# Cross-attention in one block: the order in which x's norm, the keys, values and queries, the softmax and the output projection are issued

## The reference

```
h = h + memory_cross_attention(rmsnorm(h, xa_norm_w), rmsnorm(mem, mem_norm_w), wq, wk, wv, wo)

q, k, v = hn @ wq, mn @ wk, mn @ wv                    # 4 heads x 128
scores = einsum('bshd,bmhd->bhsm', q, k) * 128 ** -0.5
probs = softmax(scores, axis=-1)
o = einsum('bhsm,bmhd->bshd', probs, v)
return o @ wo
```

## Time and profile before

| what | us |
|---|---|
| median of three runs | 2760.13 (2759.71 to 2760.22) |
| the profiled execution | 2763.47 |
| its span | 2761.8 |
| PE busy | 2337.4 (85%) |
| DVE busy | 1330.7 (48%) |
| ACT busy | 807.1 (29%) |
| POOL busy | 21.5 (1%) |

### The profile page before, as it was taken

How to read it: one execution, slowest core, us unless ns; L and a number is a source line. 1 busy time by engine, 2 the same in 40 slices (tenths; PEclk the granted TensorE clock), 3 DMA queues, 4 the chain that set the end, 5 groups by cost and what they waited for, 6 DMA issues and landing times. The chain is left out here.

```text
span 2761.8 us, 40825 instructions
## 1 busy us (share of the span) xinstructions
PE 2337.4 (85%) x17264; PEld 1888.0 (68%) x17264; DVE 1330.7 (48%) x1528; ACT 807.1 (29%) x966; POOL 21.5 (1%) x62
## 2 busy tenths in 40 slices
PE   5996659978898798699999999996978577888885
PEld 5996559958776665699999999985854433443442
DVE  3763445565525301588888879784552211111112
ACT  4443223332113301443434334434441111111110
POOL 0000000000000000000000000000000000000000
PEclk9997879978758899899999999998999568999997
DMA  4442003410004430588888888863432399999998
GB/s 177 182 182 119 2 1 122 182 54 3 2 1 163 173 122 0 232 334 332 314 327 329 317 329 331 339 229 145 183 122 89 135 370 412 428 427 427 428 428 344
DMA packets 68156, 610.12 MB, mean 221 GB/s; under 512 B 9614, under 2 KB 9870, under 8 KB 16782
## 3 DMA queue, kind: packets, MB, share of 16 engines
q1 hardware_dynamic: 56906, 572.11, 51.8%
q0 software_dynamic: 1872, 23.07, 2.1%
q10 hardware_dynamic: 9216, 12.60, 1.3%
HBM read 674.85 MB, written 14.68 MB: 250 GB/s over the span
## 5 line engine op out<-in xcount | busy, mean ns | idle before, releaser
L1759 ACT ACTIVATE ffn_w_hi<-ffn_raw 128x2048 fp32r<-128x2048 f32 x128 | 245.0, 1916 | 371.2 <-PE psum L1804 367.9
L1766 DVE TENSOR_TENSOR ffn_w_lo<-ffn_raw,ffn_w_hi 128x2048 fp32r<-128x2048 f32 x128 | 292.3, 2287 | 88.9 <-ACT ffn_w_hi L1759 88.9
L1802 PE MATMUL psum<-u_hi,ffn_w_hi 128*128 128x256 f32 x1024 | 293.5, 287 | 15.1 <-DVE ffn_w_lo L1766 14.0
L2511 PE MATMUL psum<-moe_raw,moe_x_t 128*32 128x512 f32 x1536 | 219.3, 703 | 87.6 <-DMA moe_raw<-in_moe 80.0
L1804 PE MATMUL psum<-u_hi,ffn_w_lo 128*128 128x256 f32 x1024 | 293.0, 286 | 0.0
L1803 PE MATMUL psum<-u_lo,ffn_w_hi 128*128 128x256 f32 x1024 | 292.9, 286 | 0.0
L591 DVE SCALAR_TENSOR_TENSOR shared<-mod_raw,c_silu,shared 128x2048 f32<-128x2048 f32 x96 | 225.1, 2344 | 0.0
L1802 PEld LDWEIGHTS psum<-u_hi,ffn_w_hi 128*128 128x128 f32 x1024 | 199.8, 195 | 15.9 <-DVE ffn_w_lo L1766 14.2
L1803 PEld LDWEIGHTS psum<-u_lo,ffn_w_hi 128*128 128x128 f32 x1024 | 199.6, 195 | 0.4
L1804 PEld LDWEIGHTS psum<-u_hi,ffn_w_lo 128*128 128x128 f32 x1024 | 199.6, 195 | 0.0
L1802 PE MATMUL psum<-ffn_w_hi,ffn_hid_hi 128*128 128x512 f32 x512 | 199.5, 390 | 0.0
(11 more groups left out here) (537 smaller groups left out, 4491.2 us busy)
## 6 DMA issues: line engine op xcount, KB each, us to landing
moe_raw<-in_moe SPq DMA_DIRECT2D x96, 2048.0 KB, 17.4
ffn_raw<-in_ffn SPq DMA_DIRECT2D x128, 1024.0 KB, 5.0
ring<-in_stream SPq DMA_DIRECT2D x59, 2048.0 KB, 12.3
mod_raw<-in_mod SPq DMA_DIRECT2D x96, 1024.0 KB, 7.3
moe_raw<-in_moe POOLq DMA_DIRECT2D x48, 2048.0 KB
expert_rows<-moe_stage ACTq DMA_DIRECT2D x192, 64.0 KB, 8.4
x<-in_x SPq DMA_DIRECT2D x2, 1024.0 KB, 8.0
mem<-in_mem SPq DMA_DIRECT2D x2, 1024.0 KB, 15.0
```

The source lines that it names most:

```text
L1759: act.activation(self.w_hi[:, number % self.HIGHS], self.raw[:, number % self.RAWS], ACT.Copy)\
L1766: dve.tensor_tensor(self.w_lo[:, number % self.LOWS], self.raw[:, number % self.RAWS], self.w_hi[:, number % self.HIGHS].bitcast(F32), ALU ...
L1802: pe.matmul(out, lhs[0], rhs[0], start=start, stop=False)
L2511: mm = pe.matmul(summed(tile)[strip(q), :], e.x_t[:, tile // 4 % 2, UNIT_KC * u + c, strip(tile % 4)], w[:, c * COLS:(c + 1) * COLS], star ...
```

## The change

The block for the loads of `mem` goes: they are issued in the block after the RWKV rounds, into the buffer `u`, which the mixer no longer needs then and which now lives until cross-attention ends. The memory's norm stands alone and first. Everything else becomes one block.

In it, ACT squares x and takes the root ahead of its copies of the keys, and DVE makes the diagonals. After the keys PE multiplies a matrix of ones with the diagonals: the result (`factors`) holds each token's factor on every partition. In the loop over the values' 16 chunks PE also turns the two pieces of x of that chunk (plain transposes), into the banks 0 to 3, two chunks a bank; DVE multiplies each chunk from PSUM by the norm's weight and by `factors`. Before the queries PE waits until DVE has taken all of them. Then heads are staggered: a head's scores are issued after the next head's query, and so on, with ACT's and DVE's lists in the matching order. The output projection starts with the column groups 0 and 1, head by head, between the last turns and attends.

```diff
+def marks(first, *names):
+
+    return {name: first + n + 1 for n, name in enumerate(names)}
...
-    norm_turn(nc, k, x, h_t, lambda c: col(k, "xa_norm", c))
     norm_turn(nc, k, mem, mem_t, lambda c: col(k, "mem_norm", c), await_src=mem_in)
-    f0, t0 = k.ft, k.tt
+    f0, t0, o0, turns, HEADS = k.ft, k.tt, k.tt + 2, k.turns, range(XA_HEADS)
+    on_pe = marks(k.pe_n, "factors", "scores0", "scores1", "probs_t0", "scores2", "probs_t1", "o0", "scores3",
+                  "probs_t2", "o1", "probs_t3", "o2", "o3")
+    on_act = marks(k.act_n, "x0", "x1", "root", "exp0", "exp1", "probs_t0", "exp2", "probs_t1", "o0", "exp3", "probs_t2",
+                   "o1", "probs_t3", "o2", "o3")
+    on_dve = marks(s.n, "inv", "diag0", "diag1", "factors", "max0", "top0", "inv0", "probs0", "max1", "top1", "inv1",
+                   "probs1", "max2", "top2", "max3", "top3", "inv2", "probs2", "inv3", "probs3")
+    factors = h_t[:, KC - 1, :]
+    spare = bank(k, 4 + (t0 + 2) % 4)
...
+    def turned(c):
+        return bank(k, c // 2 % 4)[:, c % 2 * T:c % 2 * T + T]
     with nc.Block(no_gpsimd_drain=True) as block:
+            for j in range(2):
+                load_next(k, sp, STREAM["xo"][0] + j, k.tt_done, o0 + 8)
...
+            def query(h):
+                pe.wait_ge(k.ft_free, f0 + 4 + h + 1)
+                for c in range(KC):
+                    w = k.ring[:, (STREAM["xq"][0] + c // UNIT_KC) % SLOTS, c % UNIT_KC, h * P:(h + 1) * P]
+                    mm = pe.matmul(bank(k, h)[:, 0:T], w, h_t[:, c, :], start=c == 0, stop=c == KC - 1)
+                mm.then_inc(k.ft_done, 1)
+
+            def score(h):
+                pe.wait_ge(k.ft_free, f0 + 4 + 4 + h + 1)
+                for t in range(TT):
+                    mm = pe.matmul(scores(h)[:, t, :], q_t[:, h, t * P:(t + 1) * P], k_t[:, h, :], start=True, stop=True)
+                mm.then_inc(k.pe_sem, 1)
+
+            def turn(h):
+                pe.wait_ge(k.dve_sem, on_dve[f"probs{h}"])
+                for n in range(4):
+                    m, t = divmod(n, TT)
+                    mm = pe.transpose(bank(k, h)[:, n * P:(n + 1) * P], probs[:, h, t, m * P:(m + 1) * P], const(k, "ident"))
+                mm.then_inc(k.pe_sem, 1)
+
+            def attend(h):
+                pe.wait_ge(k.act_sem, on_act[f"probs_t{h}"])
+                for m in range(2):
+                    mm = pe.matmul(bank(k, h)[:, 0:T], v_m[:, m, h * P:(h + 1) * P], probs_t[:, h, m, :],
+                                   start=m == 0, stop=m == 1)
+                mm.then_inc(k.pe_sem, 1)
+
+            def out(n, h):
+                unit = STREAM["xo"][0] + h // 2
+                flat = k.ring[:, unit % SLOTS].rearrange("p k n -> p (k n)")
+                at = h % 2 * 4 * COLS + n * COLS
+                pe.wait_ge(k.act_sem, on_act[f"o{h}"])
+                for t in range(TT):
+                    if h == 0:
+                        pe.wait_ge(k.tt_free, o0 + 2 * n + t + 1)
+                    mm = pe.matmul(bank(k, 4 + (o0 + 2 * n + t) % 4), o_t[:, h, t * P:(t + 1) * P], flat[:, at:at + COLS],
+                                   start=h == 0, stop=h == XA_HEADS - 1)
+                    if h == XA_HEADS - 1:
+                        mm.then_inc(k.tt_done, 1)
             feature_group(k, pe, STREAM["xk"][0], mem_t, f0)
-            token_group(k, pe, unit_rows(STREAM["xv"][0], KC), mem_t, range(KC), t0)
-            feature_group(k, pe, STREAM["xq"][0], h_t, f0 + 4)
+            pe.wait_ge(k.dve_sem, on_dve["diag1"])
+            for t in range(TT):
+                mm = pe.matmul(spare[:, t * P:(t + 1) * P], const(k, "ones"), k.diag[:, t, :], start=True, stop=True)
+            mm.then_inc(k.pe_sem, 1)
+            for unit in range(2):
+                u = STREAM["xv"][0] + unit
+                pe.wait_ge(k.loaded[u % SLOTS], 16 * (u // SLOTS + 1))
+            for t in range(TT):
+                pe.wait_ge(k.tt_free, t0 + t + 1)
+            for c in range(KC):
+                w = k.ring[:, (STREAM["xv"][0] + c // UNIT_KC) % SLOTS, c % UNIT_KC, :]
+                for t in range(TT):
+                    mm = pe.matmul(bank(k, 4 + (t0 + t) % 4), mem_t[:, c, t * P:(t + 1) * P], w,
+                                   start=c == 0, stop=c == KC - 1)
+                    if c == KC - 1:
+                        mm.then_inc(k.tt_done, 1)
+                if c < 8:
+                    if c % 2 == 0:
+                        pe.wait_ge(k.ft_free, f0 + 4 + c // 2 + 1)
+                elif c % 2 == 0:
+                    pe.wait_ge(k.turn_taken, turns + c // 2 - 3)
+                for t in range(TT):
+                    mm = pe.transpose(turned(c)[:, t * P:(t + 1) * P], x[:, t, c * P:(c + 1) * P], const(k, "ident"))
+                if c % 2:
+                    mm.then_inc(k.turned, 1)
+            for unit in range(2):
+                u = STREAM["xq"][0] + unit
+                pe.wait_ge(k.loaded[u % SLOTS], 16 * (u // SLOTS + 1))
+            pe.wait_ge(k.turn_taken, turns + 8)
+            query(0)
+            query(1)
+            score(0)
+            query(2)
+            score(1)
+            turn(0)
+            query(3)
+            score(2)
+            turn(1)
+            attend(0)
+            score(3)
+            for unit in range(2):
+                u = STREAM["xo"][0] + unit
+                pe.wait_ge(k.loaded[u % SLOTS], 16 * (u // SLOTS + 1))
+            for h in range(3):
+                out(0, h)
+                out(1, h)
+                if h < 2:
+                    turn(h + 2)
+                attend(h + 1)
+            for n in range(2):
+                out(n, 3)
+            for n in range(2, 4):
+                for h in HEADS:
+                    out(n, h)
         @block.scalar
         def _(act):
-            for n in range(8):
+            def query(h):
+                act.wait_ge(k.ft_done, f0 + 4 + h + 1)
+                act.activation(q_t[:, h, :], bank(k, h)[:, 0:T], ACT.Copy).then_inc(k.ft_free, 1)
+
+            def exps(h):
+                act.wait_ge(k.dve_sem, on_dve[f"top{h}"])
+                for t in range(TT):
+                    exp = act.activation(probs[:, h, t, :], scores(h)[:, t, :], ACT.Exp, scale=P ** -0.5,
+                                         bias=top[:, h, t:t + 1], accum_out=total[:, h, t:t + 1])
+                exp.then_inc(k.act_sem, 1)
+
+            def turned_probs(h):
+                act.wait_ge(k.pe_sem, on_pe[f"probs_t{h}"])
+                act.activation(probs_t[:, h].rearrange("p m t -> p (m t)"), bank(k, h), ACT.Copy).then_inc(k.act_sem, 1)
+
+            def attended(h):
+                act.wait_ge(k.pe_sem, on_pe[f"o{h}"])
+                act.activation(o_t[:, h, :], bank(k, h)[:, 0:T], ACT.Copy).then_inc(k.act_sem, 1)
+            for t in range(TT):
+                act.activation(h_t[:, 8 * t:8 * t + 8, :].rearrange("p a b -> p (a b)"), x[:, t, :], ACT.Square,
+                               accum_out=k.ssq[:, t:t + 1]).then_inc(k.act_sem, 1)
+            act.wait_ge(k.act_sem, on_act["x1"])
+            act.activation(k.rms[:, 0:TT], k.ssq[:, 0:TT], ACT.Sqrt, bias=k.eps[:, 0:1], scale=1.0 / D).then_inc(k.act_sem, 1)
+            for n in range(4):
                 act.wait_ge(k.ft_done, f0 + n + 1)
-                act.activation((k_t, q_t)[n // 4][:, n % 4, :], bank(k, n % 4)[:, 0:T], ACT.Copy).then_inc(k.ft_free, 1)
+                act.activation(k_t[:, n, :], bank(k, n)[:, 0:T], ACT.Copy).then_inc(k.ft_free, 1)
+            query(0)
+            query(1)
+            exps(0)
+            query(2)
+            exps(1)
+            turned_probs(0)
+            query(3)
+            exps(2)
+            turned_probs(1)
+            attended(0)
+            exps(3)
+            turned_probs(2)
+            attended(1)
+            turned_probs(3)
+            attended(2)
+            attended(3)
+            s.eng = dve
+
+            def most(h):
+                dve.wait_ge(k.pe_sem, on_pe[f"scores{h}"])
+                s.step(dve.tensor_reduce(top[:, h], scores(h), AX.X, ALU.max))
+                s.settle()
+                s.step(dve.tensor_scalar(top[:, h], top[:, h], -P ** -0.5, None, ALU.mult))
+
+            def shares(h):
+                dve.wait_ge(k.act_sem, on_act[f"exp{h}"])
+                s.step(dve.reciprocal(total[:, h], total[:, h]))
+                s.settle()
+                s.step(dve.tensor_tensor(probs[:, h], probs[:, h], total[:, h].unsqueeze(2).broadcast_to([P, TT, T]),
+                                         ALU.mult))
+            dve.wait_ge(k.act_sem, on_act["root"])
+            s.step(dve.reciprocal(k.rstd[:, 0:TT], k.rms[:, 0:TT]))
+            s.settle()
+            for t in range(TT):
+                s.step(dve.tensor_scalar(k.diag[:, t, :], const(k, "ident"), k.rstd[:, t:t + 1], None, ALU.mult))
+            dve.wait_ge(k.pe_sem, on_pe["factors"])
+            s.step(dve.tensor_copy(factors, spare[:, 0:T]))
+            s.settle()
```

(99 more changed lines are left out.)

6 lines of the change are left out of this document (2 added, 4 removed).

## The result

| what | before | after |
|---|---|---|
| runs made together, median, us | 2760.18 (2759.71 to 2763.82) | 2731.68 (2730.85 to 2734.93) |
| ratio, 95% interval | | 0.9892 (0.9879 to 0.9905) |
| the profiled execution | 2763.47 | 2731.61 |
| its span | 2761.8 | 2729.9 |
| mixer's last add ends | 933.41 | 935.45 |

Faster by 28.5 us in the medians, by 26 to 33 in the ratio's interval; forecast was 25.0. The time, 2731.7 by the medians and 2730.4 by the ratio, lies at or under the range's lower end of 2731.0. Direction, mechanism and order of size were right; the size was too small.

The account below looks back on a forecast made before the run. PE was taken to bound the stage, with 33 us of bubbles from serial hand-overs. Terms 1.4 − 0.9 + 16.6 − 1.4 − 5.2 + 14.9 gave 25.4, taken as 25.0: 2738.5 us profiled, 2735.1 median; range 2731 to 2744.

Parts of the forecast that it names:

- Block gone, 1.4 us: Cross-attention's start: without the block for loading `mem`, ACT's first square starts where SP had started, saving 1.4 us.
- Two more issues upstream, −0.9: Block after the RWKV rounds: the two issues of `mem` there make every engine wait, costing 0.9 us.
- x's norm gone, 16.6: Front of cross-attention: one whole norm leaves the path ahead of the keys, saving 16.6 us.
- The remaining norm takes the slow place, −1.4: Memory's norm, now first: runs at the first place's lower clock (0.72 against 0.78), costing 1.4 us.
- Left on PE, −5.2: Keys to queries: factors product 0.4, 32 transposes 3.6 and the wait for DVE 1.2 add 5.2 us.
- rival C: Values' stretch: PE's clock falls to half, adding 31 us, 2766 us in all; chance 0.02.
- Queries with scores and a turn: Queries' stretch: 27.6 us of queries plus 2.2 us for two heads' scores and one turn; softmax keeps up.
- Tail, 14.9: Last query matmul's issue to the last add: 37.9 us instead of 55.0, less 2.2 moved into queries, gains 14.9.
- Rival B: Staggered heads: ACT's and DVE's in-order queues fail to overlap them, 9 to 10 us more, 2745 us; chance 0.07.
- Cold restarts, −0.4: Whole stage: 0.4 us taken off the gain for PE restarting cold behind five real waits.
- half-hidden transposes: Values' stretch, range's lower end: the transposes, charged 3.6 us, partly fit into gaps left by weight loads.
- a tail at its best: Softmax and output projection, range's lower end: gain up to its bound of 16 us instead of 14.9.

Follow-up runs that it names:

- change again: The changed kernel, unedited, timed again beside the kernel before: profiled at 2731.92 us, median 2732.71, ratio 0.9883.
- long series: The changed kernel, unedited, timed a third time beside two further edited versions on one chip: median 2733.24 us, ratio 0.9889.
- the late stage: The changed kernel plus 13 ACT copies in a block behind the stage, so the rest starts at its old time: median 2760.54 us, ratio 0.9992.

## Where the prediction was right, and which step failed

Each term, with the time of the profile after.

- *Block gone, 1.4 us.* ACT's first square came 936.29 − 935.45 = 0.84 us behind the last add; before, 935.62 − 933.41 = 2.21. That is 1.37.
- *Two more issues upstream, −0.9.* From DVE's last product of the RWKV rounds to ACT's first copy of the next block: 2.15 us before, 3.13 after. Measured −1.0. With the loads back in their block it is 2.14 again.
- *x's norm gone, 16.6.* One norm less, true in size. What I didn't name is that this term needs the early load. Before, x's norm covered the landing of `mem` (13.9 and 16.0 us after the issues, ahead of its first use at 952.23); without the edit priced at +1.4 − 0.9, 14.3 us would have stayed. The sum was right, the attribution was not: of two edits that only pay together I gave all to one.
- *The remaining norm takes the slow place, −1.4. This step failed.* From the first square to the keys took 951.78 − 936.29 = 15.49 us; I had 16.25 + 0.5 = 16.75. The norm itself took 14.97, 15.41 (change again) and 15.03 (long series): near the second norm of before (14.85), though it stands in the first one's place. The granted clock of the window is 0.79, where I expected 0.72 by the earlier trace rows. The sentence that failed is "The difference is the clock (...), which belongs to the place": one execution had two values of it, and I made the worse one a rule. By the norm alone that is −0.1 to −0.6 instead of −1.4. The second profile of the kernel before refutes the rule itself: there the first norm took 15.82 us and the second, in the good place, 16.25. Its row:

```profile
958.79 10.34 PE L208 MATMUL psum<-diag,mem 128*128 128x128 f32 x64 [6.26 <-DVE diag L191]
```

  The same 64 records took 8.95 us in that place in the first profile. Nor is it how long PE had rested: 9.01 us after 20.93 us of idle time in the kernel with the loads in their old block, 9.06 after 6.56 in the change, 10.34 here after 6.26. What sets the clock of one execution there stays open.
- *Left on PE, −5.2.* Keys with factors 951.78 to 979.92: 28.14 (forecast 28.1). Values with transposes to the first query 32.34 (32.3), in it the wait for DVE 1.17 (1.2). The transposes' price is shown by the doubled ones. I misread a chunk, though: "0.86 + 0.22 us of PE per chunk" should be 1.72 + 0.22, for 27.5 us by 16 chunks is 1.72, and the starts of two chunks lie 981.86 − 979.92 = 1.94 us apart. The slip only made DVE's margin look smaller than it is, and the transposes' share of the stretch is a ninth, not a fifth. The clock stood at 1.00 throughout, so rival C fell. By the rule of the Trainium skill, "TensorE: Matmul & The Clock Gate", Part 4, that transposes don't count as PE activity, a fall was possible; this trace, with a pair of transposes in every chunk for 31 us, shows none. At a ninth of the time this is a weak test of the rule; the stretch of transposes alone in the earlier trace rows speaks more directly against it.
- *Queries with scores and a turn*: 1012.26 to 1042.13 is 29.87 (29.8).
- *Tail, 14.9.* 1042.13 to the last add's end at 1080.28: 38.15 (37.9). Waits, with the drain, of 1.01 and three of about 0.65 (1.1 and three of 0.63). Rival B fell: no head waits for its probabilities.
- *Cold restarts, −0.4.* Not seen: the clock column is 1.00 in every window from 951.4, and queries and tail came within 0.3 us of the sum.

The stage gained 172.35 − 145.17 = 27.2 us; I had 26.3 in absolute times. Less 1.0 upstream, 26.2 against my 25.4, or 25.0 after the deduction. Of these 1.2, the failed step (16.75 − 15.49 = 1.3) and the deduction (0.4) make 1.7, and the tail (0.3) and the upstream part (0.1) take back 0.4. With the second profile of the kernel before (171.3) and the second of the change (145.6) the gain is 25.7, less 1.0 is 24.7: the sum itself was as good as two executions agree. That the next stage began at 1080.62, where I had 1080.4, was luck: the stage ran shorter than summed, and its start came 2.0 us later where I had 0.9.

The medians say more: 28.5, 31.4 and 29.1 us in the three series of the change beside the kernel before, each with an interval of 3.6 to 5.0 us to either side. What the traces place is 25 to 26 us. The 2 to 6 us above that were not found, and no step of the sum can be named for them: neither profiles compared like for like (26.9) nor the late stage settles them. The profiled "before" was 3.3 us over its median, and its experts 6 us slower than another profile of it, which shows how little one execution tells at this size.

And the range: its lower end of 2731.0 allowed 4 us under the forecast, filled by errors of terms alone: 1.4 us for the norm, which came, and some 3 us for half-hidden transposes and a tail at its best, which did not. Runs of one kernel spread over 8 us, and medians of a few runs over 3 (2731.68, 2732.71, 2733.24 for the change; before 2760.18 to 2764.07). The range left no room for that beside the terms.

## What to carry to other kernels

Where a stage alternates between solid stretches of one engine and serial hand-overs, sum the new order from row starts of the old trace; it gave 146.1 us for a stage of 145.2 here. Before crediting an edit, ask what covered its transfers: a norm that is taken away may have been the cover of a load. And don't make a rule of place out of a clock that one execution shows (here its two values had changed places in the next profile); take both values as the ends of a range, and add the spread of the executions to it.

## What the hardware showed that I had not expected

- A transpose in fp32 between products of 512 columns costs 0.11 us of PE time, the same as in a row of its own; its record shows 0.273 us (values' stretch with 32 and with 64 transposes).
- One program's part of 545 us took 6 us more or less in two executions (549.5 and 543.2). With it went the clock granted in its first 100 us (0.67 or 0.81), though it had begun within 1 us of the same time.
- Behind the same serial softmax, the same 16 records took 3.69 or 5.49 us in two executions, with a granted clock of 1.00 or 0.76.
- A long rest of PE did not make the norm behind it slow: its 64 records took 9.01 us after 20.93 us of idle PE in one execution, and 10.34 after 6.26 in another.
- Five waits of 0.5 to 1.2 us did not take the clock off 1.00 anywhere in the 129 us from the keys to the stage's end.
